# A 64-token block solve for a gated delta rule, on one Trainium2 core

## What is computed

```python
kk = jnp.einsum("nbhcd,nbhed->nbhce", kc, kc)
a_mat = jnp.where(strict, bc[..., :, None] * kk * decay, 0.0) + jnp.eye(CHUNK, dtype=f32)
rhs = jnp.concatenate([vc * bc[..., None], kc * (bc * jnp.exp(gc))[..., None]], axis=-1)
sol = lax.linalg.triangular_solve(a_mat, rhs, left_side=True, lower=True)
u, w = sol[..., :dv], sol[..., dv:]
...
v_new = u_n - jnp.einsum("bhck,bhkv->bhcv", w_n, state)
```

## Time and profile before

| | us |
|---|---|
| median of 3 runs | 1621.75 (1620.79 to 1622.44) |
| the profiled execution | 1622.98 |
| its span, first to last instruction | 1621.0 |
| TensorE busy | 1327.2 (82%) |
| VectorE busy | 608.0 (38%) |
| ScalarE busy | 484.0 (30%) |
| the solve, from the first x to the last `solve_uw` | 125.85 to 191.9 |

### The profile page before, as it was taken

How to read it: one execution, slowest core, us unless ns; L and a number is a source line. 1 busy time by engine, 2 the same in 40 slices (tenths; PEclk the granted TensorE clock), 3 DMA queues, 4 the chain that set the end, 5 groups by cost and what they waited for, 6 DMA issues and landing times.

```text
span 1621.0 us, 32850 instructions
## 1 busy us (share of the span) xinstructions
PE 1327.2 (82%) x14418; PEld 1048.5 (65%) x14418; DVE 608.0 (38%) x980; ACT 484.0 (30%) x811; POOL 0.2 (0%) x4
## 2 busy tenths in 40 slices
PE   9999999999999999998876586576676667558666
PEld 9999899999999999995543343343343344334333
DVE  7967556787986778641110010010110110011001
ACT  6846467556644554530000000000000000000001
POOL 0000000000000000000000000000000000000000
PEclk9999999999999999999998898898899898899889
DMA  8442034443656655799999999999999999999997
GB/s 333 160 152 98 35 134 151 173 171 132 219 207 263 252 177 193 263 343 424 429 428 429 431 428 429 431 429 427 435 429 427 429 429 433 426 429 431 428 433 310
DMA packets 42264, 517.92 MB, mean 320 GB/s; under 512 B 4816, under 2 KB 4944, under 8 KB 7248
## 3 DMA queue, kind: packets, MB, share of 16 engines
q1 hardware_dynamic: 42048, 516.71, 78.1%
q10 hardware_dynamic: 144, 0.17, 0.0%
HBM read 515.81 MB, written 1.05 MB: 319 GB/s over the span
## 4 chain that ended last, share of the span: by engine, by line
PE 50%; DMA 42%; DVE 4%; ACT 2%; issue 1%; SPq 1%; another core or an unknown queue 0%; DVEq 0%; ACTq 0%
DMA e_gu<-experts 42%; PE psum L346 11%; PE psum L347 11%; PE psum L348 11%; PE psum L986 7%; PE psum L1030 3%; DVE w_low L1696 1%; PE psum L602 1%; PE psum L1036 1%; DVE a_gdn_qk L1745 1%; DMA w_raw<-dense 0%; PE psum L962 0%; PE psum L1016 0%; SPq L2405 0%; PE psum L587 0%
## 5 line engine op out<-in xcount | busy, mean ns | idle before, releaser
L986 PE MATMUL psum<-e_gu,x_xt 128*32 128x256 f32 x3072 | 217.9, 447 | 175.2 <-DMA e_gu<-experts 175.1
L986 PEld LDWEIGHTS psum<-e_gu,x_xt 128*32 128x32 f32 x3072 | 108.3, 128 | 277.0 <-DMA e_gu<-experts 186.9
L346 PE MATMUL psum<-h_high,w_high 128*128 128x256 f32 x864 | 245.4, 284 | 0.6 <-DVE w_low L1696 0.6
L347 PE MATMUL psum<-h_low,w_high 128*128 128x256 f32 x864 | 242.7, 281 | 0.0
L348 PE MATMUL psum<-h_high,w_low 128*128 128x256 f32 x864 | 242.6, 281 | 0.0
L1696 DVE TENSOR_TENSOR w_low<-w_raw,w_high 128x2048 fp32r<-128x2048 f32 x99 | 225.7, 2288 | 28.0 <-ACT w_high L1119 20.6
L1119 ACT ACTIVATE w_high<-w_raw 128x2048 fp32r<-128x2048 f32 x99 | 189.2, 1914 | 60.2 <-PE psum L348 50.3
L2371 DVE COPY x_yb<-psum 128x256 f32<-128x256 f32 x64 | 27.2, 424 | 423.0 <-PE psum L1030 423.0
L346 PEld LDWEIGHTS psum<-h_high,w_high 128*128 128x128 f32 x864 | 162.8, 188 | 7.1 <-issue 4.7
L347 PEld LDWEIGHTS psum<-h_low,w_high 128*128 128x128 f32 x864 | 162.8, 188 | 0.1
L348 PEld LDWEIGHTS psum<-h_high,w_low 128*128 128x128 f32 x864 | 162.8, 188 | 0.0
(11 more groups left out here) (464 smaller groups left out, 2114.6 us busy)
## 6 DMA issues: line engine op xcount, KB each, us to landing
e_gu<-experts SPq DMA_DIRECT2D x44, 4096.0 KB, 52.9
w_raw<-dense SPq DMA_DIRECT2D x100, 1024.0 KB, 4.8
e_dn<-experts SPq DMA_DIRECT2D x45, 2048.0 KB, 49.4
e_dn<-experts SPq DMA_DIRECT2D x37, 1024.0 KB, 54.8
e_gu_lo<-experts SPq DMA_DIRECT2D x16, 2048.0 KB, 51.5
e_gu_hi<-experts SPq DMA_DIRECT2D x15, 2048.0 KB, 55.9
e_gu<-experts SPq DMA_DIRECT2D x8, 1024.0 KB, 6.4
e_gu<-experts SPq DMA_DIRECT2D x2, 1536.0 KB, 8.0
```

Source lines behind the costliest of these rows:

```text
L346: mm(ps, w[0], src[0], start=start, stop=False, **kw)
L347: mm(ps, w[0], src[1], start=False, stop=False, **kw)
L986: last = mm(half(psum[32 * s:32 * s + 32, GU_BANK[j % 2], 0:256], P), X["xt"][:, k, CAP * j:CAP * (j + 1)], expert_gu(j, k)[:, :, s * P:(s ...
```

## The change

- `t`, `u`, `xx` hold 64-wide blocks: chunk `c` (0 or 1) of a token tile lies on partitions 64c to 64c+63, and a bank holds one `c` of all 8 matrices, 64 x 512. `chunk_products` fills two banks at once, with 16 matmuls of 64x64 that alternate between rows and columns 0 to 63 and 64 to 127 of the array. Both chunks of both token tiles go through each step together, so every step waits for both.
- beta goes into the start (a diagonal matrix `beta` instead of the identity), so the copies of `xx`, `v_in` are without a scale, and one copy serves a bank. `k_in` is scaled by exp of the decay alone. VectorE makes `beta` with four multiplies, and clears the 128-wide `full_u`, into which level 5 writes the inverse. `t` of level 0 is now a product.
- Gate units `ga00` and `ga01` run after x of levels 3 and 4. Their sigmoids (`gates`) run on ScalarE in levels 4 and 5. `oa_0`'s low part is made in level 3. The fox lists get an empty entry.

```diff
-        A["lm"], A["xx"] = (half(sq[:, 4 * i:4 * i + 4, :].rearrange("p a b -> p (a b)"), P) for i in range(2))
+        A["lm"] = half(sq[:, 0:4, :].rearrange("p a b -> p (a b)"), P)
+        A["full_u"] = A["u"]
+        A["beta"] = half(A["u"].rearrange("p a b -> p (a b)")[:, 0:2 * H * CHUNK], CHUNK)
+        A["u"] = half(A["t"].rearrange("p a b -> p (a b)")[:, 2 * H * CHUNK:4 * H * CHUNK], CHUNK)
+        A["solve_t"] = half(A["t"].rearrange("p a b -> p (a b)")[:, 0:2 * H * CHUNK], CHUNK)
+        A["xx"] = half(A["tmp"], CHUNK)
+        CHUNK_ROWS = tuple(slice(c * CHUNK, (c + 1) * CHUNK) for c in range(2))
...
-            def solve_x(lv, t):
-                ps = aux.fill(pe, f"x{lv}{t}")
+            def chunk_products(units, left, right):
+
+                ps = [aux.fill(pe, u) for u in units]
+                last = [None, None]
+                for un in range(2 * H):
+                    for c, rows in enumerate(CHUNK_ROWS):
+                        last[c] = mm(ps[c][rows, un * CHUNK:(un + 1) * CHUNK], left(rows, un), right(rows, un),
+                                     start=True, stop=True)
+                for c in range(2):
+                    aux.filled(last[c], units[c])
+
+            def solve_x(lv):
+                t = A["solve_t" if lv else "beta"]
                 pe.wait_ge(sem("gdn_lm"), lv + 1)
                 if lv:
-                    pe.wait_ge(sem("gdn_t"), 2 * (lv - 1) + t + 1)
-                for hd in range(H):
-                    un = t * H + hd
-                    o = ps[:, hd * P:(hd + 1) * P]
-                    if lv == 0:
-                        last = nc.tensor.transpose(o, A["lm"][:, un, :], ident)
-                    else:
-                        last = mm(o, A["lm"][:, un, :], A["t"][:, un, :], start=True, stop=True)
-                aux.filled(last, f"x{lv}{t}")
-
-            def solve_tu(lv, t):
-                pe.wait_ge(sem("gdn_xx"), 2 * lv + t + 1)
+                    pe.wait_ge(sem("gdn_t"), 2 * lv)
+                chunk_products((f"x{lv}0", f"x{lv}1"), lambda rows, un: A["lm"][rows, un, rows], lambda rows, un: t[rows, un, :])
+
+            def solve_tu(lv):
+                u = A["u" if lv else "beta"]
+                pe.wait_ge(sem("gdn_xx"), 2 * lv + 2)
                 if lv:
-                    pe.wait_ge(sem("gdn_u"), 2 * (lv - 1) + t + 1)
-                for nm in ("t", "u"):
-                    if nm == "t" and lv in (0, len(LEVELS) - 1):
-                        continue
-                    ps = aux.fill(pe, f"{nm}{lv}{t}")
-                    for hd in range(H):
-                        un = t * H + hd
-                        u = ident if lv == 0 else A["u"][:, un, :]
-                        xx = A["xx"][:, un, :]
-                        last = mm(ps[:, hd * P:(hd + 1) * P], u if nm == "t" else xx, xx if nm == "t" else u,
-                                  start=True, stop=True)
-                    aux.filled(last, f"{nm}{lv}{t}")
+                    pe.wait_ge(sem("gdn_u"), 2 * lv)
+                if lv < len(LEVELS) - 1:
+                    chunk_products((f"t{lv}0", f"t{lv}1"), lambda rows, un: u[rows, un, :], lambda rows, un: A["xx"][rows, un, :])
+                chunk_products((f"u{lv}0", f"u{lv}1"), lambda rows, un: A["xx"][rows, un, :], lambda rows, un: u[rows, un, :])
...
-                pe.wait_ge(sem("gdn_u"), 2 * (len(LEVELS) - 1) + t + 1)
+                pe.wait_ge(sem("gdn_u"), 2 * len(LEVELS))
...
-                            lambda: fox_scores(3), lambda: fox_turn(2),
+                            lambda: fox_scores(3), lambda: fox_turn(2), lambda: None,
...
-                solve_x(lv, 0)
-                solve_x(lv, 1)
+                solve_x(lv)
                 if lv == 0:
                     unit("sk1")
                 elif lv < 3:
                     unit_tok(f"sv{lv - 1}")
+                elif lv < 5:
+                    unit(f"ga0{lv - 3}")
                 between()
-                solve_tu(lv, 0)
-                solve_tu(lv, 1)
+                solve_tu(lv)
                 between()
...
-                        gate(b, hf, p)
+                        if b != "a" or hf:
+                            gate(b, hf, p)
...
-                for hd in range(H):
-                    un = t * H + hd
-                    last = ac(A["v_in"][:, un, :], ps[:, hd * P:(hd + 1) * P], ACT.Copy,
-                              scale=A["tok"][:, t, 8 + hd:9 + hd])
-                aux.emptied(last, f"turn_v{t}")
...
-            def solve_evac(lv, t):
-
-                ps = aux.wait(act, f"x{lv}{t}")
-                for hd in range(H):
-                    un = t * H + hd
-                    last = ac(A["xx"][:, un, :], ps[:, hd * P:(hd + 1) * P], ACT.Copy,
-                              scale=A["tok"][:, t, 8 + hd:9 + hd])
-                link(last)
-                aux.release(act, f"x{lv}{t}")
+                aux.emptied(ac(A["v_in"][:, t * H:(t + 1) * H, :], half(ps, P), ACT.Copy), f"turn_v{t}")
+
+            def solve_evac(lv, c):
+
+                ps = aux.wait(act, f"x{lv}{c}")
+                rows = CHUNK_ROWS[c]
+                link(ac(A["xx"][rows, :, :], half(ps[rows, :], CHUNK), ACT.Copy))
+                aux.release(act, f"x{lv}{c}")
                 act.sem_inc(sem("gdn_xx"), 1)
...
+                          lambda: softmax_exp(A["s"], A["st"], "fox", 2, FSP), lambda: None,
+                          lambda: softmax_exp(A["s"], A["st"], "fox", 3, FSP),
...
+                if lv > 3:
+                    gates("a", 0, lv - 4)
...
-            gates("a", 0, 0); o_evac(0); sb_log(0); gates("a", 0, 1); sb_log(1); sb_exp(0)
+            o_evac(0); sb_log(0); sb_log(1); sb_exp(0)
...
+            for rows in CHUNK_ROWS:
+                for t in range(TT):
+                    last = V.tensor_tensor(A["beta"][rows, t * H:(t + 1) * H, :],
+                                           ident[rows, rows].rearrange("p (a b) -> p a b", a=1).broadcast_to([CHUNK, H, CHUNK]),
+                                           A["tok"][rows, t, 8:12].rearrange("p (a b) -> p a b", b=1).broadcast_to(
+                                               [CHUNK, H, CHUNK]), ALU.mult)
+            link(last)
             lm(0)
             inverse_heads(half(A["tmp"]))
...
-            def first_t(t):
-
-                dve.wait_ge(sem("gdn_xx"), t + 1)
-                c = slice(t * H, (t + 1) * H)
-                V.tensor_tensor(A["t"][:, c, :], ident.rearrange("p (a b) -> p a b", a=1).broadcast_to([P, H, P]),
-                                A["xx"][:, c, :], ALU.subtract).then_inc(sem("gdn_t"), 1)
-
-            def solve_sub(lv, t, nm):
-                ps = half(aux.wait(dve, f"{nm}{lv}{t}"), P)
-                o = A[nm][:, t * H:(t + 1) * H, :]
-                src = ident.rearrange("p (a b) -> p a b", a=1).broadcast_to([P, H, P]) if lv == 0 else o
-                link(V.tensor_tensor(o, src, ps, ALU.subtract))
-                aux.release(dve, f"{nm}{lv}{t}")
+            def solve_sub(lv, c, nm):
+                ps = aux.wait(dve, f"{nm}{lv}{c}")
+                rows = CHUNK_ROWS[c]
+                held = A["solve_t" if nm == "t" else "u"][rows, :, :]
+                o = A["full_u"][rows, :, rows] if lv == len(LEVELS) - 1 else held
+                link(V.tensor_tensor(o, held if lv else A["beta"][rows, :, :], half(ps[rows, :], CHUNK), ALU.subtract))
+                aux.release(dve, f"{nm}{lv}{c}")
                 dve.sem_inc(sem(f"gdn_{nm}"), 1)
...
-                          lambda: (fout(1), fmax(2)), lambda: (fnorm(2), fmax(3)), lambda: fnorm(3), lambda: fout(2),
+                          lambda: (fout(1), fmax(2)), lambda: (fnorm(2), fmax(3)), lambda: None, lambda: fnorm(3), lambda: fout(2),
...
-                if lv < 3:
-                    lows(("sv0", "sv1", "ga01")[lv])
+                if lv < 4:
+                    lows(("sv0", "sv1", "ga01", "oa_0")[lv])
...
-                for t in range(TT):
-                    for nm in ("t", "u"):
-                        if nm == "t" and lv == 0:
-                            first_t(t)
-                        elif nm == "u" or lv < len(LEVELS) - 1:
-                            solve_sub(lv, t, nm)
+                for nm in ("t", "u"):
+                    for c in range(2 if nm == "u" or lv < len(LEVELS) - 1 else 0):
+                        solve_sub(lv, c, nm)
+                if lv == 0:
+                    link(V.memset(A["full_u"], 0.0))
                 between()
...
-            lows("oa_0")
```

46 lines of the change are left out of this document (21 added, 25 removed).

## The result

| | us, median (lowest to highest) | ratio to before, 95% |
|---|---|---|
| before | 1621.32 (1620.19 to 1622.76), 20 runs | |
| after | 1623.55 (1621.99 to 1625.69), 20 runs | 1.0013 [1.0007, 1.0019] |
| forecast | 1618.8 (1613.5 to 1626.0) | |

The time lies inside the range, and the difference is within the 0.2% that counts as no change, but its sign is certain and is not the one forecast. The profiled execution of after took 1622.16 us, against 1622.98 for that of before; the forecast for it was 1620.0.

The account below looks back on a forecast made before the run. TensorE bounds the solve (busy 54.82 of 57.50 us) as long as no other engine is waited for. Solve lead 5.8, less 1.95 after it, 0.6 for edges and 0.3 for the clock: 3.0 us gained, 1618.8 us, range 1613.5 to 1626.

Parts of the forecast that it names:

- level 1's turn copy: Level 1 of the solve: TensorE idle from 147.8 to 149.95 before u, waiting for ScalarE's copy of fox turn 0.
- level 5's copies and subtractions: Level 5: waits for two ScalarE copies (1.5 us with links) and, after u, two subtractions (1.75 us).
- the state copies: After the solve: TensorE idles 1.65 us before the state product, until VectorE has done keep and four copies.
- The half clock at the end of the solve: Behind level 5's idle of 3.3 us, TensorE's clock falls to half, costing 1.5 us.
- edges: Where TensorE meets blocks of another shape: about 0.1 us a block, 12 blocks, half behind a wait, 0.6 us.
- rival 1: In the solve the array's two places take turns, so every product costs 1.8 us as before: 1628.4 us, chance 0.13.
- rival 3: The clock never falls and edges cost nothing, 4 us more kept: 1614.8 us, chance 0.17.
- rival 4: The end does not follow, because the expert stream began as early anyway: 1621.8 us, chance 0.03.
- the price of a product: In the solve, 32 records over two simultaneous places take 0.9 us; 17 products take 15.3 us, against 28.7 before.
- The lead at the end of the solve: solve_uw ends at 197.5 against 203.3, a lead of 5.8 us.
- Rival 2: Longer waits, more clock falls or edges that drain TensorE fully lose 3 us: 1621.8 us, no change, chance 0.27.
- a solve longer than 75 us: Sign of a wrong forecast: x of level 0 to the end of solve_uw over 75 us, where 70.9 was expected.

Follow-up runs that it names:

- experiment 4: The changed kernel with each product's matmuls reordered, all of chunk 0 and then all of chunk 1: 1631.7 us, ratio 1.0061.
- experiment 11: Both kernels unaltered, profiled again: before 1620.33 and 1620.41 us; after 1622.52, 1622.89 and 1624.13 us.
- experiment 9: Before's 128-column products with gate units in halves, state copies ahead of sb_keep(0), turned fox tile first in level 1: 1618.27 us, ratio 0.9979.
- experiment 3: Before's kernel with 128-column products and only the gate units moved into levels 3 and 4, their sigmoids after the solve: 1624.98 us, ratio 1.0022.
- experiment 8: The changed kernel with gate units in halves, state copies ahead of sb_keep(0), and turned fox tile first in level 1: 1615.0 us, ratio 0.9961.
- experiment 2: The changed kernel with 64-wide products but the gate units, their sigmoids and oa_0's low part back after the solve: 1626.65 us, ratio 1.0032.

## Why the prediction was wrong

**What held.** The mechanism, nearly wait by wait. Forecast and measured (us): beta 0.5 and 0.35; level 0's bank 0.7 and 0.30; level 1's turn copy 2.15 and 1.96; x of level 2 0.8 and 0.69; x of level 5 1.2 and 0.78; level 5's copies and subtractions 1.5 + 1.75 and 1.54 + 2.22; `vnew` 0.65 and 0.50; the state copies 1.65 and 1.80. The text of the forecast does not name the 0.96 us ahead of x of level 4, but its ends of x leave 0.9 us open there (9.65 us, less a unit of 5.7, a turn of 0.33 and three products). The half clock at the end of the solve cost 1.7 us where 1.5 was counted. The two places work at once (experiment 4), clock and edges are not free, and the end follows the landmark: rivals 1, 3 and 4 fall.

**The step that failed inside the profiled execution: the price of a product.** Ends of x by level:

| | x1 | x2 | x3 | x4 | x5 | `solve_uw` |
|---|---|---|---|---|---|---|
| forecast | 140.85 | 153.55 | 167.2 | 176.85 | 188.25 | 197.5 |
| measured | 140.5 | 153.8 | 167.8 | 178.2 | 190.1 | 200.3 |

The error grows from level to level; only in the last step, with one product, are the waits (0.5 us) and the clock (0.2 us) more of it than the product. From first record to the next instruction, waits taken off, the 17 products take 18.7 us, 1.1 each. The sum had 17 x 0.9 = 15.3 us and 0.6 for the edges: 2.8 us too little. The lead at the end of the solve, the edges taken off, was forecast at 5.2 us and found at 3.0 (203.3 - 200.3): 2.2 less, since the waits came out 0.8 us shorter in all and the half clock took 0.2 more. Which part of the price was missed? The 0.9 was 32 x 55 / 2. Experiment 4 shows that halving was right, and that the pace of one place is 58 ns, not 55: the first and the last start of a product lie 0.88 to 0.93 us apart, 15.8 us in all 17. The rest, 2.9 us, lies between the last start of a product and the next instruction, 0.05 to 0.22 us each time (waits taken off), and against that the sum had only the 0.6 for edges. Even where no other shape follows, between t and u, it is 0.12 us (135.80 to 135.92), so this is not a matter of changed shapes alone; what makes it is not shown. On full edges the trace sides with the rows: 0.20 us instead of 0.11 into a block (146.47 to 146.67), not a drained array.

After the solve the loss was 2.5 us (from 3.0 us of lead to 213.97 - 213.43 = 0.54 at the sums), 0.5 more than the 1.95 of the forecast. Together: 3.0 us forecast, 0.54 found at the sums, 0.82 in the time of the execution.

**The step that failed outside it: one execution taken for the kernel.** The forecast ended "1620.0; against the median of 1621.75 it is 1618.8", a shift of 1.2 us down. In the runs the profiled execution of after is 1.4 us below its median, so this step alone is off by 2.6 us, about as much as the first. Experiment 11 shows where most of that is from: by the landmark, the first profile of before is 0.9 us later than the mean of its four (266.99 and 266.1), that of after 0.9 us earlier than the mean of its five (266.45 and 267.4). The execution of before that I read had a clock fall at level 3 that two of its four profiles lack; the sum credited the change with removing it (the earlier trace rows stand in level 3's working) although two of the four profiled executions had nothing there to remove. The execution of after has 3.4 us of half clock, the least of its five, as one other has. By the mean landmarks after is 1.3 us behind, 0.4 of it ahead of the first x, by the medians of the runs 2.2; the 0.9 between them is not settled by nine profiles.

Rival 2, longer waits or more falls, 1621.8, came nearest: three of after's five profiles have half clock for twice as long behind level 5, one of them behind level 1 as well. The waits themselves were not longer, but for those of level 5 (3.76 us for 3.25). The prediction's own sign of being wrong, a solve longer than 75 us, shows in these three (75.1 to 76.0); in the first profile it is 74.3, where 70.9 was forecast. From an execution of before without a fall (landmark 265.2) the same sum has 1.6 us less to win, 1.4 in all, and with 2.8 us more for the products it is a loss of 1.4; the landmarks of after are 1.3 to 3.3 us behind that one.

**Where the gain is.** The wide products of experiment 9 take 27.5 us in all (15 at 1.78 and the transposes of level 0, 0.8), the narrow ones of after 18.7. Of these 9 us 1.4 reach the time with the units as placed (experiment 3 against after), and 3.3 once the longest waits have work in them or a better order (experiments 8 and 9). The gate units as placed fill level 3, which has 4.1 us open without them (0.58 and 3.52, experiment 2), and level 4, which has 0.8; they leave 3.8 us at level 5 and 1.8 behind the solve.

## What to carry to other kernels

A shorter product on an engine that alternates with evacuations turns into waits; count the waits behind each step, and place filler of their size at each rather than a whole unit at two of them. Before taking an execution as the base of a sum, ask whether a clock fall in it belongs to the kernel or to that execution; a wait of the same length can have either behind it. The pace of the records inside a group is not the price of the group: here the pace was forecast within 3 ns, and most of what was missed stands between one group and the next, 0.17 us on the mean, 17 times.
